# Moving the third layer's modulation sums to VectorE, and reordering four places of a four-layer backbone kernel

## The reference, cut to what matters

```python
for i in range(DEPTH):
    shift_x, scale_x, gate_x = jnp.split((sc @ mod_w[i] + mod_b[i])[:, None, :], 3, axis=-1)
    shift_c, scale_c, gate_c = jnp.split(scc @ mod_w[i] + mod_b[i], 3, axis=-1)
    hx = x * (1.0 + scale_x) + shift_x
    hc = ctx * (1.0 + scale_c) + shift_c
    out_x, out_c = mixer_i(hx, hc, ...)
    x = _layer_norm(DEEPNORM_ALPHA * x + gate_x * out_x, ln_g[i], ln_b[i])
```

## Time and profile before

| | us |
|---|---|
| device time, median of 3 runs (lowest to highest) | 1456.61 (1455.66 to 1457.94) |
| device time of the profiled execution | 1452.48 |
| its span, first to last instruction | 1451.2 |
| PE matmul busy | 1376.4 (95%), 8233 instructions |
| PEld busy | 1137.7 (78%) |
| DVE busy | 1134.3 (78%), 1664 instructions |
| ACT busy | 716.2 (49%) |
| POOL busy | 296.0 (20%) |
| read from HBM | 208.75 MB, 145 GB/s over the span |

### The profile page before, as it was taken

One profiled execution on the slowest core, in us unless ns is written; L12 is line 12 of the kernel. 1 busy time (PEld: TensorE's weight loads), 2 busy tenths in 40 slices (PEclk: granted clock), 3 DMA queues, 4 the chain that ended last, 5 costly groups with the idle time before them and its releaser, 6 DMA issues.

```text
span 1451.2 us, 21790 instructions
## 1 busy us (share of the span) xinstructions
PE 1376.4 (95%) x8233; PEld 1137.7 (78%) x8233; DVE 1134.3 (78%) x1664; ACT 716.2 (49%) x1231; POOL 296.0 (20%) x324
## 2 busy tenths in 40 slices
PE   3799999999989999999899999999999999999987
PEld 2788888888867799776578878888788788888875
DVE  0699988988984568767748779888438999999996
ACT  1565666565662353545544332323334666665562
POOL 1033333344241021001000000000001243344350
PEclk8999999999999999999999999999999999999999
DMA  9257655676644312324332346354531455655553
GB/s 351 74 173 200 191 160 167 184 220 179 180 154 158 118 48 88 117 85 164 131 118 85 99 135 204 125 164 155 187 117 31 123 131 151 154 132 132 145 162 142
DMA packets 135864, 211.71 MB, mean 146 GB/s; under 512 B 9744, under 2 KB 102864, under 8 KB 135760
## 3 DMA queue, kind: packets, MB, share of 16 engines
q1 hardware_dynamic: 121616, 163.08, 35.4%
q0 software_dynamic: 12096, 44.34, 12.2%
q10 hardware_dynamic: 2048, 2.90, 0.6%
HBM read 208.75 MB, written 1.54 MB: 145 GB/s over the span
## 4 chain that ended last, share of the span: by engine, by line
PE 70%; DVE 15%; ACT 7%; issue 3%; DMA 2%; SPq 2%; POOL 1%; ACTq 0%; DVEq 0%; POOLq 0%
PE ps L482 19%; PE ps L484 19%; PE ps L483 19%; DVE w_lo L451 2%; PE ps L702 2%; PE ps L513 2%; DVE xc L1020 2%; PE ps L2103 1%; ACT Wb L877 1%; PE ps L2087 1%; DVE stats L1894 1%; DVE resid L1890 1%; DVE ps L1887 1%; PE ps L693 1%; PE ps L665 1%
## 5 line engine op out<-in xcount | busy, mean ns | idle before, releaser
L482 PE MATMUL ps<-h_hi,w_hi 128*128 128x512 f32 (+2 forms) x1088 | 407.7, 375 | 13.2 <-DVE w_lo L451 7.2
L484 PE MATMUL ps<-h_hi,w_lo 128*128 128x512 f32 (+2 forms) x1088 | 397.7, 365 | 0.0
L483 PE MATMUL ps<-h_lo,w_hi 128*128 128x512 f32 (+2 forms) x1088 | 397.4, 365 | 0.0
L451 DVE TENSOR_TENSOR w_lo<-raw,w_hi 128x1024 fp32r<-128x1024 f32 (+1 forms) x203 | 247.8, 1242 | 117.0 <-ACT w_hi L442 116.9
L442 ACT ACTIVATE w_hi<-raw 128x1024 fp32r<-128x1024 f32 (+1 forms) x203 | 207.3, 1051 | 151.8 <-PE ps L484 116.6
L482 PEld LDWEIGHTS ps<-h_hi,w_hi 128*128 128x128 f32 (+1 forms) x1088 | 204.9, 188 | 47.9 <-issue 11.8
L484 PEld LDWEIGHTS ps<-h_hi,w_lo 128*128 128x128 f32 (+1 forms) x1088 | 204.8, 188 | 33.3
L483 PEld LDWEIGHTS ps<-h_lo,w_hi 128*128 128x128 f32 (+1 forms) x1088 | 205.1, 189 | 31.3
L1020 DVE SCALAR_TENSOR_TENSOR xc<-ps,gp,xc 128x508 f32<-128x508 f32 (+1 forms) x224 | 161.4, 726 | 16.8 <-ACT xc L828 12.1
L484 PE MATMUL ps<-w_hi,ylo 128*128 128x512 f32 x376 | 148.8, 396 | 0.0
L482 PE MATMUL ps<-w_hi,h_hi 128*128 128x512 f32 (+1 forms) x336 | 118.8, 354 | 6.7 <-DVE w_lo L451 3.3
(11 more groups left out here) (282 smaller groups left out, 2456.3 us busy)
## 6 DMA issues: line engine op xcount, KB each, us to landing
raw<-in_mod_w SPq DMA_DIRECT2D x80, 512.0 KB, 4.4
raw<-in_ssm_w_in SPq DMA_DIRECT2D x64, 512.0 KB, 6.4
cum_b<-cum_scratch POOLq DMA_DIRECT2D x48, 512.0 KB, 9.5
raw<-in_ssm_w_in SPq DMA_DIRECT2D x66, 256.0 KB, 5.3
raw<-in_ssm_w_out SPq DMA_DIRECT2D x32, 512.0 KB, 4.6
raw<-in_pool_w_in SPq DMA_DIRECT2D x32, 512.0 KB, 4.4
raw<-in_attn_w_in SPq DMA_DIRECT2D x20, 512.0 KB, 3.8
raw<-in_pool_w_out SPq DMA_DIRECT2D x16, 512.0 KB, 4.2
```

The costliest lines, as they stand in the source:

```text
L451: dve.tensor_tensor(lo, w_shaped(key, raw[:, r % RS, :], width), hi.bitcast(F32), ALU.subtract).then_inc(lo_done, 1)
L482: pe.matmul(o, hi_s, hi_m, start=first, stop=False)
L483: pe.matmul(o, hi_s, lo_m, start=False, stop=False)
L484: return pe.matmul(o, lo_s, hi_m, start=False, stop=last)
```

## The change

It has these parts; the diff below is cut to them.

1. L2's 24 units are summed by DVE, in three sums of eight. The first goes into L0's output chunks 4 to 11 (one unit behind each weight split; accumulated in `pr`, `prT`), the second into the attention layer (three units before the loop; five in the loop, each cut in two halves ahead of and behind `divide`; in `gate_b`), the third into the pool layer's first groups. L3's sums move on by one: two in the pool layer's later groups, the third in the pool layer's output chunks 4 to 11 (in `Hs`, `xw`), folded in the norm behind it. PE's 12 slots in the attention loop go; the folds are three more.
2. In the attention loop gate products and weight splits on DVE move from behind `divide` to behind `maxima`, splits into the next pair.
3. Pool layer: the z weights are split at tile 0 and not 1; the gate row is made in group 3.
4. Head: all 16 units are loaded ahead of the first weights; tiles are scaled, rounded and finished in halves of four column blocks, and PE's first projection begins with the first half.
5. End of L0's scan: chunks 2 and 3 of the output projection go behind the last scan matmuls, step 8's units for L1 are loaded in one piece, and DVE's and ACT's orders are rewritten.
6. L3: in each step the next group's first x split goes ahead of a tap and the z splits one tap later; in the last step PE turns two tiles, projects, and then turns the third, and DVE and ACT follow.

```diff
     MOD_SUMS = [[(0, 0, 8), (1, 0, 8), (2, 0, 4), (2, 4, 8)],
                 [(part, k, k + 4) for part in range(MOD_PARTS) for k in (0, 4)],
-                [(0, 0, 4), (0, 4, 8), (1, 0, 6), (1, 6, 8), (2, 0, 8)],
+                [(part, 0, 8) for part in range(MOD_PARTS)],
                 [(part, 0, 8) for part in range(MOD_PARTS)]]
...
+    POOL_SUMS = [(2, 2), (3, 0), (3, 1)]
...
+    def out_units(L):
+        return {0: units_of(2, 0), 2: units_of(3, 2)}.get(L, [])
...
+    ATTN_FIRST = 3
+    ATTN_AT = {(0, 4): 3, (0, 5): 4, (1, 4): 5, (2, 1): 6, (2, 3): 7}
...
+    def mod_acc(L, n, v):
+        if (L, n) == (2, 0):
+            return (pr[:, :, :].rearrange("p a n -> p (a n)"), prT[:, :, :, :].rearrange("p a k n -> p (a k n)"))[v]
+        if (L, n) == (3, 0):
+            return (lng_b, lnb_b)[v][:, :]
+        if (L, n) == (3, 2):
+            return (Hs, xw)[v][:, 0:2, :, :].rearrange("p k d n -> p (k d n)")
+        return gate_b[:, v, :]
...
+        if last_layer(L):
+            pe_turn_tiles(pe, L, g, (0, 1))
+            ssd_project(pe, L, GRP, 5)
+            pe_turn_b(pe, L, g)
+        else:
+            pe_turn_inputs(pe, L, g)
+            ssd_project(pe, L, GRP, 5)
...
         pe_scan_ctx(pe, L, g)
-        stage_a(pe, L, 0)
+        stage_a(pe, L, 0, (0, 1))
         if mods:
             pe_mod_units(pe, *mods, units[2:], 6)
         stage_a(pe, L, 1, (0, 1))
         pe_scan_lat(pe, L, g, mods)
+        stage_a(pe, L, 0, (2, 3))
         stage_a(pe, L, 1, (2, 3))
...
         if not has_in and last_layer(L):
+            turned((0, 1))
             dx()
-            turned()
+            turned((2,))
...
             gate(i - 2, 0)
             gate(i - 2, 1)
+            for c in (0, 1):
+                dve_split(dve, L, "out", c, 0)
+            halve()
             decay(0)
-            decay(1)
-            halve()
             for c in (0, 1):
                 dve_ylo(dve, L, c)
-            for c in (0, 1):
-                dve_split(dve, L, "out", c, 0)
+            decay(1)
...
             halve()
             for c in (0, 1):
                 dve_split(dve, L, "out", c, 0)
+            decay(2)
             state(0)
-            state(1)
             mix(0)
             mix(1)
+            state(1)
             state(2)
-            for c in range(4):
+            for c in (0, 1):
                 dve_ylo(dve, L, c)
-            decay(2)
-            for c in (2, 3):
-                dve_split(dve, L, "out", c, 0)
             decay(3)
-            y_ctx(g)
             mix(2)
             if mods:
                 dve_mod_col(dve, *mods, 6)
             mix(3)
+            y_ctx_intra(g)
+            for c in (2, 3):
+                dve_ylo(dve, L, c)
+                dve_split(dve, L, "out", c, 0)
+            y_ctx_scaled(g)
+            y_ctx_inter(g)
             y_lat(g)
...
             next_x = ("x", i + 1) if i + 1 < GRP else ("z", i)
+            dve_split(dve, L, *next_x, 0)
             tap(3, 0)
-            dve_split(dve, L, *next_x, 0)
             tap(3, 1)
...
+    def pe_head_begin(pe):
+        for half in range(2):
+            pe_tiles_ready(pe, 0, half + 1)
+            ssd_pe_dt(pe, 0, 0, SEG, (4 * half, 4 * half + 4))
+            project(pe, bank[0], (0, "x", 0), 0, None, 0, SEG, (4 * half, 4 * half + 4))
...
             pe_begin(pe, L + 1, 0)
+            if L == 2:
+                pe_mod_fold(pe, 3, 2, 2)
             pe_turn(pe, s, N - 1, N - 1, (s["xhat_d"], s["base"]["xhat_d"] + N))
...
         dve_affine_half(dve, s, 3, tiles[3])
+        if L == 2:
+            dve_mod_col(dve, 3, 2, 2)
         dve_h_lo(dve, s, 3, tiles[3])
...
-            if more:
-
-                if mod_slot(g, slot) is not None:
...
-                    pe_mod_units(pe, L + 1, n, layer_units(L + 1)[2 * q:2 * q + 2], 5)
+            if (g, slot) == (3, 1):
+                pe.wait_ge(s["turned_a"], 3 * NKV)
+                pe_mod_fold(pe, 2, 1, 5)
...
             tok_tile(pe, (0, 1), (L, "k", 0), tt, s["kv_p"])
+        pe_mod_fold(pe, 2, 0, 4)
...
         dve_split2(dve, L, "q", 0)
+        dve_mod_unit(dve, attn_units()[0])
         norm_sum(0)
+        dve_mod_unit(dve, attn_units()[1])
         norm_scale(0)
...
+                if g < 3 and m == 5:
+                    gate_product(g + 1, g // 2)
+                if g == 2 and m == 3:
+                    gate_product(3, 0)
+                if (g, m) == (3, 1):
+                    dve_mod_col(dve, 2, 1, 5)
+                if divmod(n - 1, NPAIR) in SPLIT_AT:
+                    dve_split(dve, L, *SPLIT_AT[divmod(n - 1, NPAIR)])
+                if (g, m) in ATTN_AT:
+                    dve_mod_half(dve, attn_units()[ATTN_AT[g, m]], 0)
...
                 divide(n)
+                if (g, m) in ATTN_AT:
+                    dve_mod_half(dve, attn_units()[ATTN_AT[g, m]], 1)
...
-                if more and g >= 2 and t == 0:
+                if g >= 2 and t == 0:
                     pe.wait_ge(s["mix_d"], 4 * g)
-                    pe_mod_fold(pe, L + 1, g - 2, 6)
+                    pe_mod_fold(pe, *POOL_SUMS[g - 2], 6)
+                    if g == 3:
+                        pe_gate(pe, L)
...
-                if t == 1:
+                if t == 0:
                     dve_split2(dve, L, "z", (g, 0))
...
         for c in range(4, 12):
             dve_split(dve, L, "out", c, 0)
+            dve_mod_unit(dve, out_units(L)[c - 4])
...
-        for u in range(HEAD_UNITS - 4):
+        for u in range(HEAD_UNITS):
             load_head(u)
         for r, (kind, n, key) in enumerate(items):
-            if r == 2:
-                for u in range(HEAD_UNITS - 4, HEAD_UNITS):
-                    load_head(u)
...
                 for c in (8, 9, 14, 15, 10, 11) if last_layer(L) else range(4, 12):
                     dve_split(dve, L, "out", c, 0)
+                    if out_units(L):
+                        dve_mod_unit(dve, out_units(L)[c - 4])
```

282 lines of the change are left out of this document (147 added, 135 removed).

## The result

The changed kernel takes 1429.34 us (median of four runs, 1428.43 to 1431.72) against 1456.13 for the kernel before on the same chip: ratio 0.9817, 95% interval 0.9800 to 0.9834. Its profiled execution took 1429.7 us for a span of 1428.4. The forecast was 1427.0 in a range of 1416 to 1441, so the time and the direction are right. The working behind it is right in some terms and clearly wrong in others, and that is what this part is about.

What follows compares the result with a forecast made beforehand. PE was taken as the bound (busy 1376.4 of 1451.2 us). Terms -14.3, -3.0, -4.6, -4.4 and -3.3 sum to -29.6: 1452.5 becomes 1422.9, plus 4.1 to reach the median gives 1427.0, range 1416 to 1441.

Steps and rivals of the forecast that it cites:

- parts 1 and 2: Attention layer: modulation sums and their waits leave PE, and DVE's loop is reordered; -14.3 us together with the folds.
- The order's -1.9: Attention loop: with maxima ahead of gate products and splits, PE's 2.75 us wait for exponentials at 706.83 shrinks to about 1.
- The halves, taken as 0 in bounds 0 to 6.4: Attention loop: five units summed on DVE in halves around the division cost nothing, at most 5 x 1.28 = +6.4 us.
- the clock's 1.6: Attention loop: PE's low clock from 708.2 to 711.4 loses 1.6 us; left in the sum, though it might go with its waits.
- What the last group gives back: Attention loop's last group, 704 to 742: of five 1.0 us slots removed, +2.4 us is given back (bounds 0 and +5).
- Pool layer (-3.0, and +0.4 for the fold): Pool layer: earlier z split removes two PE waits of 1.5, -3.0 us (0 to -3.5); fold in the norm behind, +0.4.
- Head (-4.6): Head: units loaded in a row save 3.0 us, tiles finished in halves save 1.6; -4.6 in all (0 to -6.5).
- End of L0's scan (-4.4): End of L0's scan, 407 to 437: DVE limits and its idle 5 us can go, one wait stays; -4.4 us (-1 to -6.5).
- L3 (-3.3): L3: six steps lose a 0.47 us DVE tap ahead of x's split, -2.8; last step 0.5; total -3.3 us (-1 to -6).
- That DVE bounds the loop: Rival, attention loop: DVE becomes the bound, busy 102 of 114 us; price +6.4 and +2.6, giving 1436 us; chance 0.22.
- That the new orders bring little: Rival: waits in pool layer, head, L0's scan end and L3 return one instruction later; 1438.5 us; chance 0.10.
- The ring: Rival, output chunks of L0 and pool layer: four slots starve them; 1464 us at a 12 us landing; chance 0.02.

## Why the prediction was right, and where it wasn't

**Attention (parts 1 and 2, -14.3 with the norm's fold).** The stretch fell by 14.2; the fold in the norm behind the pool layer stands in *pool*, so the forecast for the stretch alone was -14.7. The mechanism holds: PE executes no sum there any more (192 rows fewer on that line, folds from 48 to 96), and the loads' waits are gone. The terms beside it were off and nearly cancel. The order's -1.9 was about right against the trace of before, where its wait shrank by 2.2 (2.91 to 0.75), but it is worth 3.7 in waits and up to 3.2 through the clock beside the new halves: it is also what keeps them from delaying the exponentials. The halves, taken as 0 in bounds 0 to 6.4, cost 1.9, and my reason (a pair is five times as long as a half) says too little: twice as much costs 10.3. The wait for the bank at 719.36 was put down as saved whole (2.26, 2.4 from start to start); 1.0 was saved, since PE now waits 1.4 for exponentials at the like place, 702.94. And the clock's 1.6 came on top. What the last group gives back (forecast 2.4): from the same matmul on, 701.96 before, it took 40.2 us, and takes 33.2 now (690.43 to 723.60). Five slots, 2.2 and 1.0 of waits that shrank, and 1.6 of clock, less 1.0 for the fold that now stands in it at 696.81, make 8.8; 7.0 came. So 1.8 was given back.

**The clock.** I left the dip of the earlier trace rows in the sum. In the profile of the changed kernel it is gone, and the old order brought it back with its wait, at twice the length. By the rule of the Trainium skill that I cited (TensorE: Matmul & The Clock Gate, What's actually happening) the dip goes with its waits. The traces agree only in part: with that wait at 0.75 and not 2.91, six of ten executions have no dip in the attention stretch, and four still have one of 3.4 us (see the last section). And another came at 412.5, at the end of L0's scan, where before there was none. It cost nothing: *L0 end* is 42.2 with it, and 42.2 to 42.3 in the executions in which the clock fell elsewhere or not at all; DVE and POOL set the end there. And in L3 I had overlooked one: before, the clock was at 0.50 from 1391 to 1394, on the last step's output chunks.

**Pool layer (-3.0, and +0.4 for the fold).** The stretch holds both: forecast -2.6, measured -2.63. Undoing the split's place alone costs 2.96, which leaves 0.3 for the fold and the gate row. Right in size and cause.

**Head (-4.6).** The steps hold: loads 2.3 to 3.1 (3.0), halves 1.7 (1.6). The first projection starts at 41.24, not at 40.5 (40.5 to 42.4 in the 12 executions). The pair of profiles shows only 3.1 in all, because the head varies by 2 us between executions (82.75 to 80.58 with the same instructions), part of it by the clock: low from 40.4 to 47.2 in the changed kernel, under 6.0 us of projections, and from 42.5 to 49.3 before, under 4.2. The median of the 12 new heads, 81.2, is 4.0 under the one head that I have of before.

**End of L0's scan (-4.4).** Wrong in size and mechanism: -1.5. The step that failed is *"its idle 5 us is what can go"*. DVE's idle time didn't go, it moved: 5.0 of 30 us before, 5.2 of 28 after. The new wait of 3.85 is for POOL's third weighting. That is not late by its own input, which ACT has ready at 411.1; it stands behind POOL's addition of squares, which waits for ACT's square at 415.1, and that comes behind ACT's splits and exponentials. I looked at DVE's and PE's queues, but not at POOL's.

**L3 (-3.3).** The stretches give -1.6. Steps: -3.0 (forecast -2.8), right in size, but the cause named is at most one of two: undoing the tap alone costs nothing, see above. Last step: forecast 0.5 by DVE, measured +1.6 with the tail. The text had it (*"what PE saves there it waits for later"*, and PE waiting in the output chunks as a sign of being wrong) but not its price. DVE, which was full before and after (15.35 and 15.65 of 16 us), didn't keep up with PE's gain, so the last slots come free 3 us later against PE; and the rows that POOL loads there, as it did before and which the text didn't mention at all, leave no room on the DMA engines (0.91 busy from 1388 to 1400) to make that up. Two of them moved away give 2.9 back. Why DVE takes 1.5 to 1.8 us longer to its splits, with either order of the last step, stays open.

**The splits moved in that step** took 3.18 us for two before and take 3.18 now: they were moved, and POOL's weighting had moved too. DVE and POOL instruction for instruction, the changed kernel:

```profile
1357.20 3.18 DVE L473 TENSOR_TENSOR w_lo<-raw,w_hi 128x1024 fp32r<-128x1024 f32 x2
1360.31 0.41 DVE L1100 TENSOR_TENSOR bt_cb<-ps,half 128x256 f32<-128x256 f32 x1
1360.64 1.29 DVE L1086 TENSOR_TENSOR cum_b<-cum_b,sg 128x1024 f32<-128x1024 f32 x1
1361.97 0.98 DVE L1091 TENSOR_TENSOR cum_b<-cum_b 128x512 f32<-128x512 f32 x1
1362.88 2.25 DVE L1649 SCALAR_TENSOR_TENSOR ylo<-ys,par,h_hi 128x256 fp32r<-128x256 f32 x2
1365.05 2.32 DVE L1086 TENSOR_TENSOR cum_b<-cum_b,sg 128x1024 f32<-128x1024 f32 x1
```

```profile
1356.39 7.04 POOL L1363 TENSOR_TENSOR xw<-xT,sg 128x256 f32<-128x256 f32 x6 [5.50 <-ACT xT L912]
1363.39 2.89 POOL L1372 TENSOR_TENSOR Wb<-Wb,bt_cb 128x512 f32<-128x512 f32 x2
```

While POOL is busy, from 1356.4 to 1366.2, the splits take 3.18 for two (2.35 without it), the roundings 2.25 for two (0.87 at 1372.72 without it). The sum of -4.0 for this part supposed that the splits get out of POOL's way; it did not come, since they didn't. The rule beside it, of the Trainium skill (SBUF — State Buffer, Who interferes with whom), is that a DVE instruction with two SBUF inputs contends with a GpSimd one that reads SBUF; the trace agrees, by the times just given.

**The rivals.** That DVE bounds the loop cost 1.9 of the 9.0 us of its price. That the new orders bring little was half true: of 15.3 for parts 3 to 6, the profiles show 3.0 + 3.1 + 1.5 + 1.6 = 9.2. The ring didn't starve: *chunks, norm* is 83.8 in nearly all executions, as before.

**The sum.** Forecast 29.6, measured between the profiles 22.8. Missing are 2.9 (L0's end), 1.7 (L3), 1.5 (head), 0.5 (attention) and 0.2 (chunks and norm): 6.8. That 1427.0 came within 2.3 of the median, 1429.3, is luck in part. Between the profiles the forecast is off by 6.8. The 4.1 was added because the profiled execution of before was that much under its median; with the fourth run it is 3.6, and the changed kernel's was 0.3 above its own. So the medians differ by 26.8, and the miss there is 2.8.

## What to carry to other kernels

An engine's idle time is not a gain in waiting: price the next thing that it will wait for, through the queue of every engine in that chain. When a stage ends the program, look at what else is due on the DMA engines there (rows that a later step needs, loaded by another queue), and issue it where they are idle; here 1 MB moved forward by two steps was worth 2.9 us, as much as the reordering of that layer's steps (3.0). And where two causes are put forward for one short wait, undo each alone and both together: either may be enough. Before you credit a wait that is gone to an edit, see whether a low clock ahead of it only hides it.

## What was not expected of the hardware

The same instructions meet low clock in different places from one execution to the next. The attention stretch with its new order has 1.2 GHz somewhere between 703 and 711 in four of ten executions (254.2 to 254.3 us) and nowhere in the other six (253.35 to 253.39): 0.9 us. The same at L3's start, 59.9 instead of 58.3 in three of 13, with the clock low for 3.4 us just there (1130.3 to 1133.7 in one of them). Such a dip of 3.4 us cost 1.6 at L3's start, 0.9 in attention, and nothing at the end of L0's scan, where PE doesn't set the pace. A single pair of profiles can thus show a gain or a loss of 1 to 2 us that belongs to neither kernel; the stretch in several runs tells.

Not tried: POOL's third and fourth weighting ahead of its squares at the end of L0's scan, which by an estimate from the rows above would free DVE's mixing some 4 us sooner; and the five units of the loop in L1's output chunks, worth at most the 1.9 us that leaving them out brought.
